# The turned x kept in memory by thirds, in place of turning it a second time

## The chip, the cores and the metric

The kernel runs on one core of one Trainium2 chip. The metric is the device time of one execution in microseconds. Engines are named as the profile names them: PE (TensorE), DVE (VectorE), ACT (ScalarE), POOL (GpSimd) and SP (SyncE, which only issues DMAs here).

## The reference, cut to what matters

```python
proj = x @ w_in                      # x: 1024 prompt + 128 sample tokens, 1024 wide
qa, ka, va, fa, qb, kb, vb, rb, a1, ga, gb = split(proj)
oa = fox_mixer(qa, ka, va, logsigmoid(fa + b_fgate), past)     # forgetting attention, 8 heads x 64
ya = oa @ w_a_out
ob = gla_mixer(qb, kb, vb, logsigmoid(a1 @ w_a2 + b_a2) / 16)  # gated linear attention, 4 heads
yb = (rms(ob) * g_gla * silu(rb)) @ w_b_out
x1 = LN(alpha * x + (sigmoid(ga) * ya + sigmoid(gb) * yb) @ w_o)
up = x1 @ w_up                        # then causal convolution, GEGLU, w_down, LN, per-layer embedding, LN
```

The prompt (1024 tokens) attends to itself; each of 8 sample streams (16 tokens each) attends to 256 cached keys and to its own. x is needed as the left side of every column of proj. The columns qa, ka, va, fa and a1 are computed ahead of the attention, all the others behind it.

## The kernel before, in words

Every float32 product is made of three matmuls: each operand is split into a part rounded to fp32r (`x_hi`) and the remainder (`x_lo`), and hi·hi, hi·lo and lo·hi are added in PSUM. ACT makes the rounded parts, DVE the remainders.

**x.** PE contracts over partitions, so x must lie with its 1024 features on partitions. For each of the 9 token tiles SP loads 128 rows (512 KB), PE turns them with 8 transposes of 128x128 (`turn_x`, L714 to L718), ACT copies the bank as `x_hi` (L1318, through L1300) and DVE subtracts for `x_lo` (L1901 to L1906). The two parts fill R1 and R2, each [128, 3 thirds, 8, 384 tokens]. A third is 3 tiles.

**Order of the work.** All is written out by hand, each engine its own program in order, and held together by semaphores. PE does: turn x, the columns of `w_in` that attention needs (loads 0 to 11, `load(n)`, L2905), then the prompt's attention head by head (`scores`, `probs_v`, L864), then the sample stage, then the gated linear attention (qb and kb first) and the rest. From the prompt's attention on, R1 and R2 hold that attention's operands, so x is gone when qb is wanted.

**The second turn.** SP therefore loads the 9 tiles of x again (`x_again`, L2996), the first four while the prompt's attention still runs, the others behind it, each as soon as its buffer is free. PE turns tile TURN_X2[0] behind the last `probs_v`, tiles 1 to 5 of that list inside the sample stage, and the last three (tiles 0, 1, 2: third 0) behind it. ACT and DVE split each again.

**The sample stage** (L946 to L960) is a loop over b = 0 to 10, software pipelined. In turn b PE does `past_keys(b+1)` (L886, 8 transposes), `sample_out(b-3)` (L934), a tile of x where 0 < b < 6, `sample_scores(b)` (L685, 20 matmuls with those of `sample_v`), `sample_turn(b-1)` (L920) and `sample_v(b-2)`. At b = 8, 9 and 10 a third of qb or kb is made (`QB_EARLY`), from thirds 2 and 1 of x. Then third 2 of kb, a wait for wa2 and for `s_a1`, and third 0 of qb and kb. `s_a1` comes from ACT, which copies the rank-16 input of the decay once POOL has stored the sample streams' output (L2761).

**PSUM.** It is four slots of two banks. `take` (L385 to L392) gives them out: with no slot named, use number i gets slot i modulo 4; before a use PE waits until every earlier use of that slot has been drained by its readers. `copied` waits for a use to have been drained, `past_pe` for PE to have filled it, `product` is the reader's side. The up projection is the first to name its slots: `first_half(0, 0)` asks for slot 0, `turn_x1(7)` for 3, `first_half(1, 0)` for 1. Just before it come, with no slot named, the alternating uses of the output projection and of the transposes of x1, in this order: wo(1, 6), x1T(4), wo(1, 7), x1T(5), wo(1, 8), x1T(6). The last two fall on slots 0 and 1: there are 514 uses before `first_half(0, 0)`, nine of which are the second turn's. DVE drains wo(1, 8) in L1882 (alpha·x added) and x1T(6) in L2345 (the remainder of x1's tile 6), which in its program comes behind the layer norm of tile 8.

Of the kernel before, what the change touches and what calls it, by code (L numbers as in the profile page):

```python
# [88 lines left out]
def build(nc, x_prompt, x_sample, cache_fox_k, cache_fox_v, cache_fox_logf, state_gla, cache_ffn_conv,  # L89
# [4 lines left out]
    with ctx:  # L94
# [149 lines left out]
        X_BUFS = 7  # L244
        xs = at(off["xs"], X_BUFS, 1024)

        TURN_X2 = [6, 7, 8, 3, 4, 5, 0, 1, 2]
        X2_HOME = {6: 0, 7: 1, 8: 2, 3: 3, 4: 4, 5: 0, 0: 1, 1: 2, 2: 3}
        x2_homes = [at(off["va"] + 1024 * i, 1024) for i in range(4)] + [at(off["qT"], 1024)]
        xs2 = [x2_homes[X2_HOME[n]] for n in range(NT)]  # L250
        qT, kT, va = at(off["qT"], 4, T), at(off["kT"], 4, T), at(off["va"], NT, 512)
        cwT = at(off["cw"], 4, 44)
        cacheT = at(off["cacheT"], 44, 16)
# [59 lines left out]
        x1h, x1l = rounded("x1_hi", off["x1h"], KT, T), rounded("x1_lo", off["x1l"], KT, T)  # L313
        g1, b1 = at(off["g1"], D), at(off["b1"], D)

        oa_out = nc.dram_tensor("branch_a", (P, 4, T), F32).ap()
        rs_out = nc.dram_tensor("row_sums", (H_A, SEQ), F32).ap()
        ri_out = nc.dram_tensor("row_scales", (H_A, SEQ), F32).ap()
# [217 lines left out]
        s_g1 = sem("ln_gains_in")  # L536

        s_xh1 = sem("x_hi_ready")
        s_sm = sem("small_hi_ready")
        s_sl = sem("small_lo_ready")  # L540
        s_obs = sem("branch_b_stored")
# [138 lines left out]
        def _(pe):  # L680
# [193 lines left out]
            turn_max(0)  # L874
            for u in range(3, 6):
                row_scores(1, u)
            def turn_again(n):
                pe.wait_ge(s_xt[n], 32)
                turn_x("xT2", n, xs2[n])

            def past_keys(b):
                pe.wait_ge(s_kp[b % 4], 16 * (b // 4 + 1))
# [52 lines left out]
                m.then_inc(filled(("soT", b)), 1)  # L935

            pe.wait_ge(s_ex, NT_S)
            turn_again(TURN_X2[0])
            pe.wait_ge(s_oe, 2 * H_A)
            pe.wait_ge(s_cols, 48)  # L940
            for b in range(DEC_B + 3):
                if 1 < b + 1 < DEC_B:
                    past_keys(b + 1)
                if b in QB_EARLY:
                    g = QB_EARLY[b]
                    copied(pe, *[("xT2", n) for n in range(3 * g, 3 * g + 3)])  # L946
                    thirds(("qb", 0), ("qb", 0), x_parts, only=(g,))
                if b == DEC_B + 2:
                    thirds(("kb", 0), ("kb", 0), x_parts, only=(1,))
                if b >= 3:  # L950
                    sample_out(b - 3)
                if 0 < b < 6:
                    turn_again(TURN_X2[b])
                if b < DEC_B:
                    sample_scores(b)
                if 1 <= b <= DEC_B:
                    sample_turn(b - 1)
                if 2 <= b <= DEC_B + 1:
                    sample_v(b - 2)
            for n in TURN_X2[6:]:  # L960
                turn_again(n)
            thirds(("kb", 0), ("kb", 0), x_parts, only=(2,))
            copied(pe, *[("xT2", n) for n in TURN_X2[6:]])

            pe.wait_ge(s_b, 16 * 2)
            pe.wait_ge(s_a1, 1)
# [323 lines left out]
        def _(act):  # L1290
# [106 lines left out]
            for q in range(2):  # L1397
                for n in range(NT):
                    o = product(act, ("va", q, n))
                    if q == 0:  # L1400
                        if n == 0:
                            act.wait_ge(s_nc0, 2)
                        copy(fat[:, n, 0:H_A], o[:, 256:256 + H_A])
                        copy(fat[:, n, 32:48], o[:, 256 + H_A:W_VF])
                    copy(va[:, n, q * 256:(q + 1) * 256], o[:, 0:256]).then_inc(drained(("va", q, n)), 1)
                    if (q, n) == (0, 2):
                        split_hi(11)
                    if (q, n) == (0, NT - 1):
                        forget_logs()
                    if (q, n) == (1, 1):  # L1410
                        decay_rank()
                    if (q, n) == (1, 2):
                        copied(act, *[("qa", 0, g) for g in range(3)])
                        qk_hi(0)

            def past_turned(b):
# [37 lines left out]
            for b in range(DEC_B + 1):  # L1454
                if 1 < b + 1 < DEC_B:
                    past_turned(b + 1)
                if b < 6:
                    x_hi("xT2", TURN_X2[b])
                if b in (DEC_B - 1, DEC_B):
                    split_hi(12 + b - DEC_B + 1)  # L1460
                if b >= 1:
                    o = product(act, ("spt", b - 1))
                    if b >= 3:
                        past_pe(act, ("spv", b - 3))
                    copy(sPT[:, (b - 1) % 2, :], o[:, 0:384]).then_inc(drained(("spt", b - 1)), 1)
                if b < DEC_B:
                    act.wait_ge(s_smx, b + 1)
                    if b >= 2:
                        past_pe(act, ("spt", b - 2))
                    o = product(act, ("ss", b))  # L1470
                    act.activation(sP[:, b % 2, 256:384], sN[b % 2], ACT.Exp, bias=nm[:, b % 2:b % 2 + 1],
                                   accum_out=rsb[:, b % 2:b % 2 + 1])
                    act.activation(sP[:, b % 2, 0:256], o[:, 0:256], ACT.Exp, bias=nm[:, b % 2:b % 2 + 1],
                                   accum_out=rs[:, b % 2:b % 2 + 1]).then_inc(s_exs, 1)
# [12 lines left out]
            split_hi(14)  # L1487
            qb_third(0, 1)
            copied(act, *[("spv", b) for b in range(DEC_B)])
            x_hi("xT2", *TURN_X2[6:])  # L1490
            copied(act, *[("soT", b) for b in range(DEC_B)])
            act.wait_ge(s_oao, 64)
            act.wait_ge(s_oas2, 32 * 2 * H_A + 16)
# [378 lines left out]
        def _(dve):  # L1872
# [162 lines left out]
            for b in range(DEC_B + 3):  # L2035
# [8 lines left out]
                if b >= 3:  # L2044
# [1 line left out]
                    t = 16 * (b - 3)  # L2046
                    dve.tensor_copy(oas[:, :, t:t + 16], o[:, 0:64].rearrange("p (j t) -> p j t", j=4))\
                        .then_inc(drained(("soT", b - 3)), 1)
                if b < 6:
                    x_lo("xT2", TURN_X2[b])  # L2050
                if b < DEC_B:
                    o = product(dve, ("ss", b))
                    q, qi = slice(b % 2, b % 2 + 1), slice(b % 4, b % 4 + 1)
# [20 lines left out]

            copied(dve, *[("soT", b) for b in range(DEC_B)])
            split_lo(14)
            x_lo("xT2", *TURN_X2[6:])
            kb_third(0, 2)

            dve.wait_ge(s_qbd, DEC_B)  # L2080
# [588 lines left out]
        def _(pool):  # L2669
# [5 lines left out]
            for i in range(2):  # L2675
                pool.memset(VH[i][:, :, DH:DH + 1].bitcast(F32), 1.0).then_inc(s_pz, 1)
                pool.memset(VL[i][:, :, DH:DH + 1].bitcast(F32), 0.0).then_inc(s_pz, 1)
            for i in range(3):
                pool.wait_ge(s_pz, 4 * i + 4)
                past_pe(pool, ("va", 1, 3 * i + 2))  # L2680
                pool.memset(sets[i][2][64:P, :].bitcast(F32), 0.0).then_inc(s_pz, 1)
                pool.memset(sets[i][3][64:P, :].bitcast(F32), 0.0).then_inc(s_pz, 1)
                pool.wait_ge(s_pz, 4 * i + 6)
                pool.memset(sets[i][2][64:66, :].bitcast(F32), 1.0).then_inc(s_pz, 1)
                pool.memset(sets[i][3][96:98, :].bitcast(F32), 1.0).then_inc(s_pz, 1)
# [77 lines left out]

            pool.wait_ge(s_oas2, 32 * 2 * H_A + 16)
            pool.wait_ge(s_oao, 64)
            past_pe(pool, *[("xT2", n) for n in range(NT)])
            pool.memset(qsm, 0.0).then_inc(s_pool, 1)
            for h in range(H_B):
                if h:
# [125 lines left out]
        def _(sp):  # L2895
# [33 lines left out]
            with nc.allow_non_contiguous_dma(reason="small columns"):  # L2929
# [3 lines left out]
                sp.dma_start(cwst[:, 0:3, :], conv_w[0].rearrange("j (c p) -> c j p", p=P)).then_inc(s_cv, 16)  # L2933
                sp.dma_start(cwst[:, 3, :], conv_b[0].rearrange("(c p) -> c p", p=P)).then_inc(s_cv, 16)
                sp.dma_start(lfp.rearrange("p (b n) h -> p b n h", n=2), cache_fox_logf[0].rearrange("b (n p) h -> p b n h", p=P)).then_inc(s_lf, 16)
            load(4)
            load(5)
            sp.dma_start(hc, consts[:, C_OMASK:C_SCAN]).then_inc(s_cols, 16)
            with nc.allow_non_contiguous_dma(reason="small columns"):
                sp.dma_start(ba2, b_a2[0].rearrange("(c p) -> p c", p=P)).then_inc(s_cols, 16)  # L2940
                sp.dma_start(ggla, g_gla[0].rearrange("(c p) -> p c", p=P)).then_inc(s_cols, 16)
                sp.dma_start(bfg, b_fgate[0].partition_broadcast(P)).then_inc(s_small, 16)
                past_pe(sp, "cacheT")
                for c, w, col in ((2 * P, H_A, O_F), (2 * P + H_A, RANK, O_A1)):
                    sp.dma_start(vfr[:, :, c:c + w], w_in[0].rearrange("(k p) n -> p k n", p=P)[:, :, col:col + w]).then_inc(s_small, 16)
            load(6)
            load(7)
            for n in range(8, 12):
                load(n)

            rows_p, rows_s = (lambda ap: ap[0, 0].rearrange("t h d -> t (h d)")), (lambda ap: ap[0].rearrange("b t h d -> (b t) (h d)"))
            def head_operands(h, parts="hl"):
# [15 lines left out]
                if "l" in parts:  # L2968
                    sp.wait_ge(s_lo, 2 * j + 2)
                    for dst, src in ((qq[DH:P], q_lo), (kc[0:DH], k_lo)):  # L2970
                        sp.dma_start(dst, src).then_inc(s_set[h % 3], 16)

            sp.wait_ge(s_ncl, 1)
            sp.wait_ge(s_hi, 3)
            head_operands(0, "h")
# [17 lines left out]
                    sp.dma_start(buf[b].rearrange("p (n c) -> p n c", n=2),  # L2993
                                 src[0, b].rearrange("(n p) h d -> p n (h d)", p=P)).then_inc(s[b % 4], 16)

            def x_again(*tiles):  # L2996
                for n in tiles:
                    sp.dma_start(xs2[n], tokens(x_prompt[0], x_sample, n)).then_inc(s_xt[n], 16)

            k_part, v_part = (kp, cache_fox_k, s_kp), (vp, cache_fox_v, s_vp)  # L3000
            for g in range(H_A):
# [15 lines left out]
            sp.wait_ge(s_s2, NS * (H_A - 1))  # L3017
            for b in range(4, 8):
                past(b, v_part)
            sp.wait_ge(s_vl, H_A)  # L3020
            sp.wait_ge(s_ov, 32)
            x_again(6, 7, 8, 3)
            sp.wait_ge(s_pv, NT_S)
            x_again(4)
            for n, after in ((5, 6), (0, 7), (1, 8), (2, 3)):
                past_pe(sp, ("xT2", after))
                x_again(n)
            past_pe(sp, ("spv", 3))
            load(14)
            load(15)  # L3030
            past_pe(sp, ("kpT", DEC_B - 1))
            load(12)
            load(13)
            copied(sp, *[("soT", b) for b in range(DEC_B)], ("spv", DEC_B - 1))
            sp.dma_start(wa2, w_a2[0]).then_inc(s_b, 16)
            sp.dma_start(scanm, consts[:, C_SCAN:C_ALL]).then_inc(s_b, 16)
# [168 lines left out]
```

## Time and profile before

| | |
|---|---|
| median of 3 runs | 2298.22 us (2296.01 to 2298.61) |
| the profiled execution | 2298.97 us |
| its span in the trace | 2297.2 us |
| mean granted clock | 0.991 |
| PE busy | 2236.4 us, 97% |
| DVE, ACT, POOL busy | 52%, 35%, 19% |
| DMA | 219.38 MB, 95 GB/s |

All stretches are us from the span's start. The prompt's attention lies at about 145 to 351, the sample stage at 351 to 446, the up projection begins at 1350.86. "Granted clock" is 1.00 where TensorE was given 2.4 GHz and 0.50 where it was given 1.2 GHz.

### The profile page before, as it was taken

How to read it: one execution, taken by the hardware profiler on the slowest of the kernel's cores; microseconds unless marked ns; L12 is line 12 of the kernel's file. 1: busy time of each engine (PE TensorE's matmuls, PEld its weight loads, DVE VectorE, ACT ScalarE, POOL GpSimd, SP SyncE). 2: the span in 40 equal slices, each digit the busy share in tenths (PEclk: the TensorE clock that was granted, in tenths of full speed). 3: DMA queues.
4: the chain of work that ended last, by engine and by line, in shares of the span. 5: the costliest groups of instructions: out<-in, count | busy, mean ns of one | idle time of the engine just before them, and what ended most of it. 6: DMA issues, size and time to landing. Idle time of an engine off the chain costs nothing.

```text
span 2297.2 us, 33210 instructions
## 1 busy us (share of the span) xinstructions
PE 2236.4 (97%) x13703; PEld 2065.8 (90%) x13703; DVE 1183.2 (52%) x1631; ACT 796.9 (35%) x1213; POOL 434.8 (19%) x537
## 2 busy tenths in 40 slices
PE   8999999999999999999999998999999999999997
PEld 8997777898999999999999888999999998888886
DVE  2226663263636363101533588666676766656446
ACT  3124664242425243112312024344444345333311
POOL 0001123001010101000032124354545420001011
PEclk9999999999999999999999999999999999999999
DMA  5109643301212121312323121222222249444420
GB/s 165 44 19 246 174 144 116 89 19 40 76 40 76 40 76 40 117 37 81 93 75 119 38 101 58 74 73 77 70 77 74 73 128 321 163 141 164 150 76 37
DMA packets 201004, 219.38 MB, mean 95 GB/s; under 512 B 40522, under 2 KB 161590, under 8 KB 200198
## 3 DMA queue, kind: packets, MB, share of 16 engines
q1 hardware_dynamic: 191846, 187.38, 26.9%
q0 software_dynamic: 9008, 29.87, 4.0%
q8 instruction: 109, 1.79, 0.3%
q14 instruction: 41, 0.34, 0.0%
HBM read 163.03 MB, written 41.53 MB: 89 GB/s over the span
## 4 chain that ended last, share of the span: by engine, by line
PE 87%; DVE 4%; SPq 2%; DMA 2%; issue 2%; ACT 1%; POOL 1%; DVEq 0%; POOLq 0%; ACTq 0%
PE ps L685 41%; PE ps L1166 19%; PE ps L1197 10%; PE ps L1245 4%; PE ps L1098 3%; PE ps L1009 2%; PE ps L864 1%; SPq L2967 1%; DVE sb L1882 1%; PE ps L824 1%; PE ps L717 1%; DVE sb L1986 1%; PE ps L1060 0%; PE ps L846 0%; PE ps L1039 0%
## 5 line engine op out<-in xcount | busy, mean ns | idle before, releaser
L685 PE MATMUL ps<-x_hi,ring_hi 128*128 128x384 f32 x960 | 326.9, 341 | 0.4 <-ACT sb L1300 0.4
L685 PE MATMUL ps<-x_hi,ring_lo 128*128 128x384 f32 x960 | 321.5, 335 | 0.0
L685 PE MATMUL ps<-x_lo,ring_hi 128*128 128x384 f32 x960 | 321.5, 335 | 0.0
L1300 ACT ACTIVATE sb<-ps 128x64 f32<-128x64 f32 (+8 forms) x235 | 106.1, 473 | 351.9 <-PE ps L685 218.2
L1896 DVE TENSOR_TENSOR ring_lo<-ring_raw,ring_hi 128x1024 fp32r<-128x1024 f32 (+1 forms) x66 | 76.0, 1158 | 210.1 <-ACT ring_hi L1300 209.2
L685 PEld LDWEIGHTS ps<-x_hi,ring_hi 128*128 128x128 f32 x960 | 180.7, 188 | 3.8 <-issue 3.5
L685 PEld LDWEIGHTS ps<-x_lo,ring_hi 128*128 128x128 f32 x960 | 180.9, 188 | 1.0 <-issue 0.7
L685 PEld LDWEIGHTS ps<-x_hi,ring_lo 128*128 128x128 f32 x960 | 180.7, 188 | 0.0
L1197 PE MATMUL ps<-down_hi,h_hi 128*128 128x512 f32 x396 | 155.6, 393 | 0.5 <-DVE h_lo L2475 0.4
L1197 PE MATMUL ps<-down_hi,h_lo 128*128 128x512 f32 x396 | 154.3, 390 | 0.0
L1197 PE MATMUL ps<-down_lo,h_hi 128*128 128x512 f32 x396 | 154.2, 389 | 0.0
L1882 DVE SCALAR_TENSOR_TENSOR convolved_halves<-sb,convolved_halves 128x1168 f32<-128x1168 f32 x88 | 127.0, 1444 | 35.5 <-ACT convolved_halves L1713 32.8
L2813 POOL TENSOR_SCALAR sb<-sb 128x1 f32<-128x1 f32 x27 | 35.4, 1312 | 443.9 <-DVE sb L2323 435.0
L2473 DVE TENSOR_TENSOR down_lo<-down_raw,down_hi 128x1024 fp32r<-128x1024 f32 x66 | 80.6, 1221 | 59.8 <-ACT down_hi L1300 59.6
L1713 ACT ACTIVATE convolved_halves<-sb 128x1168 f32<-128x1168 f32 x44 | 60.0, 1367 | 144.2 <-issue 92.0
L1882 DVE SCALAR_TENSOR_TENSOR sb<-sb 128x1024 f32<-128x1024 f32 (+5 forms) x79 | 87.5, 1118 | 38.1 <-ACT sb L1516 24.4
L685 PE MATMUL ps<-ring_hi,x_hi 128*128 128x256 f32 x360 | 104.9, 291 | 0.0
L685 PE MATMUL ps<-sb 128*128 128x256 f32 (+4 forms) x400 | 101.8, 391 | 0.1
L685 PE MATMUL ps<-ring_hi,x_lo 128*128 128x256 f32 x360 | 101.8, 283 | 0.0
L685 PE MATMUL ps<-ring_lo,x_hi 128*128 128x256 f32 x360 | 101.7, 283 | 0.0
L1300 ACT ACTIVATE down_hi<-down_raw 128x1024 fp32r<-128x1024 f32 x66 | 69.7, 1056 | 71.9 <-DMA down_raw<-in_w_down 71.8
L1882 DVE SCALAR_TENSOR_TENSOR sb<-sb,ps 128x256 f32<-128x256 f32 (+2 forms) x87 | 49.8, 595 | 79.5 <-PE ps L1098 43.8
(353 smaller groups left out, 5722.3 us busy)
## 6 DMA issues: line engine op xcount, KB each, us to landing
down_raw<-in_w_down SPq DMA_DIRECT2D x66, 512.0 KB, 3.7
ring_raw<-in_w_in SPq DMA_DIRECT2D x50, 512.0 KB, 3.9
h_raw<-h_chunks SPq DMA_DIRECT2D x66, 192.0 KB, 3.8
sb<-in_x_prompt SPq DMA_DIRECT2D x24, 512.0 KB, 7.9
h_chunks<-convolved_halves SPq DMA_DIRECT2D x22, 512.0 KB, 2.8
up_raw_b<-in_w_up SPq DMA_DIRECT2D x38, 256.0 KB, 3.8
up_raw<-in_w_up SPq DMA_DIRECT2D x34, 256.0 KB, 3.0
branch_b<-sb POOLq DMA_DIRECT2D x4, 1152.0 KB, 7.2
```

What stands on the lines that cost most here:

```text
L685: m = mm(out, l, r, start=(n == 0), stop=(n == len(pairs) - 1))
L1009: m = mm(o[:, n * w:(n + 1) * w], a[:, t], later(c, t, l), start=True, stop=True)
L1098: m = mm(o[:, 0:512], a, b, start=(k == i == 0), stop=(k == KT - 1 and i == 2))
L1166: m = mm(o[:, 512 * j:512 * j + BW], a, b[:, BW * j:BW * (j + 1)], start=(not more and k == n == 0), stop=(k == 3 and n == 2), skip_group_ ...
L1197: m = mm(o[:, cc], a, b, start=(k == e == 0), stop=(k == LAST and e == 2), skip_group_check=True)
L1245: m = mm(o, l, r, start=(k == e == 0), stop=(k == KT - 1 and e == 2))
L1300: return act.activation(out, in_, ACT.Copy, scale=scale)
L1713: act.activation(y[:, v, 0:1168], U[:, v, 0:1168], ACT.Identity, bias=cwT[:, 3, n:n + 1], scale=cwT[:, 0, n:n + 1])\
L1882: return dve.scalar_tensor_tensor(out=out, in0=in0, scalar=scalar, in1=in1, op0=op0, op1=op1)
L1896: dve.tensor_tensor(ringl[:, i, 0:kt], ring[:, i, 0:kt], ringh[:, i, 0:kt].bitcast(F32), ALU.subtract)\
L2473: dve.tensor_tensor(wdl[s % WD_SLOTS], rawd[s % WD_SLOTS], wdh[s % WD_SLOTS].bitcast(F32), ALU.subtract).then_inc(s_dl, 1)
L2813: pool.tensor_scalar(lve[:, q:q + 1], mv[:, q, 1:2], LN_EPS, None, ALU.add).then_inc(s_msq, 1)
```

## The change: what it does

After x has been turned the first time, SP stores both parts to a scratch tensor in device memory, six stores of 1536 KB (12,288 contiguous bytes in each of 128 partitions). Those who write over R1 and R2 later (ACT before `qk_hi(0)`, POOL before the memsets of the sets, SP before `head_operands`) first wait for all six. The second loads, transposes and splits go. SP loads the parts back instead: thirds 2 and 1 behind the last probabilities of the prompt's attention (each: hi whole, lo in two halves), third 0 in three pieces behind `spv` 5, 6 and 7. PE waits for the landings (`x_back`) where it waited for the splits.

```diff
+        x_out = nc.dram_tensor("x_parts", (2, 3, P, KT, THIRD), F32).ap()
...
-            def turn_again(n):
-                pe.wait_ge(s_xt[n], 32)
-                turn_x("xT2", n, xs2[n])
+            def x_back(g):
+                for n in range(3 * g, 3 * g + 3):
+                    pe.wait_ge(s_xt[n], 32)
...
             pe.wait_ge(s_ex, NT_S)
-            turn_again(TURN_X2[0])
             pe.wait_ge(s_oe, 2 * H_A)
...
                 if b in QB_EARLY:
                     g = QB_EARLY[b]
-                    copied(pe, *[("xT2", n) for n in range(3 * g, 3 * g + 3)])
+                    x_back(g)
                     thirds(("qb", 0), ("qb", 0), x_parts, only=(g,))
...
-                if 0 < b < 6:
-                    turn_again(TURN_X2[b])
...
-            for n in TURN_X2[6:]:
-                turn_again(n)
             thirds(("kb", 0), ("kb", 0), x_parts, only=(2,))
-            copied(pe, *[("xT2", n) for n in TURN_X2[6:]])
+            x_back(0)
...
# ACT
+                        act.wait_ge(s_xst, 96)
                         qk_hi(0)
...
-                if b < 6:
-                    x_hi("xT2", TURN_X2[b])
...
-            x_hi("xT2", *TURN_X2[6:])
...
# DVE
-                if b < 6:
-                    x_lo("xT2", TURN_X2[b])
...
-            x_lo("xT2", *TURN_X2[6:])
...
# POOL
+            pool.wait_ge(s_xst, 96)
...
-            past_pe(pool, *[("xT2", n) for n in range(NT)])
...
# SP
+            def x_away(g):
+                copied(sp, *[("xT", n) for n in range(3 * g, 3 * g + 3)])
+                for i, a in enumerate((xh, xl)):
+                    sp.dma_start(x_out[i, g], a[:, g].bitcast(F32)).then_inc(s_xst, 16)
...
+            x_away(0)
             load(6)
             load(7)
+            x_away(1)
+            x_away(2)
...
+            sp.wait_ge(s_xst, 96)
             sp.wait_ge(s_ncl, 1)
             sp.wait_ge(s_hi, 3)
             head_operands(0, "h")
...
-            def x_again(*tiles):
-                for n in tiles:
-                    sp.dma_start(xs2[n], tokens(x_prompt[0], x_sample, n)).then_inc(s_xt[n], 16)
+            def x_in_again(i, g, k0, k1, n):
+                sp.dma_start((xh, xl)[i][:, g, k0:k1].bitcast(F32), x_out[i, g, :, k0:k1]).then_inc(s_xt[n], 16)
...
-            sp.wait_ge(s_vl, H_A)
-            sp.wait_ge(s_ov, 32)
-            x_again(6, 7, 8, 3)
             sp.wait_ge(s_pv, NT_S)
-            x_again(4)
-            for n, after in ((5, 6), (0, 7), (1, 8), (2, 3)):
-                past_pe(sp, ("xT2", after))
-                x_again(n)
+            for g in (2, 1):
+                x_in_again(0, g, 0, KT, 3 * g)
+                x_in_again(1, g, 0, KT // 2, 3 * g + 1)
+                x_in_again(1, g, KT // 2, KT, 3 * g + 2)
...
+            past_pe(sp, ("spv", 5))
+            x_in_again(0, 0, 0, KT // 2, 0)
+            past_pe(sp, ("spv", 6))
+            x_in_again(0, 0, KT // 2, KT, 1)
+            past_pe(sp, ("spv", 7))
+            x_in_again(1, 0, 0, KT, 2)
             copied(sp, *[("soT", b) for b in range(DEC_B)], ("spv", DEC_B - 1))
             sp.dma_start(wa2, w_a2[0]).then_inc(s_b, 16)
             sp.dma_start(scanm, consts[:, C_SCAN:C_ALL]).then_inc(s_b, 16)
```

## Rows read from the trace of the kernel before

**Rows 1.** The page, part 4: the chain that ended last, shares by engine.

```profile
PE 87%; DVE 4%; SPq 2%; DMA 2%; issue 2%; ACT 1%; POOL 1%; DVEq 0%; POOLq 0%; ACTq 0%
```

**Rows 2.** Chain of waits, end of the prompt's attention: start us, us, what.

```profile
339.99 5.40 DMA row_sums<-sb
...
351.00 0.90 PE ps L717 x8
351.89 3.91 PE ps L685 x20
```

**Rows 3.** Timeline of ACT there: start, us, operation [idle before <-releaser].

```profile
345.48 0.60 ACT L1300 ACTIVATE sb<-ps 65x512 f32<-65x512 f32 x1 [2.02 <-DMA row_sums<-sb]
...
351.03 0.59 ACT L1300 ACTIVATE sb<-ps 65x512 f32<-65x512 f32 x1 [0.42 <-PE ps L864]
```

**Rows 4.** DMA view, whole span: issues, KB each, median us to landing.

```profile
row_sums<-sb POOLq DMA_DIRECT2D x16, 2.0 KB, 2.6
...
ob_raw<-branch_b POOLq DMA_DIRECT2D x3, 1536.0 KB, 7.3
```

**Rows 5.** Chain of waits, sample stage.

```profile
356.82 0.87 PE ps L717 x8
...
390.81 0.87 PE ps L886 x8
...
400.69 0.87 PE ps L886 x8
...
407.15 2.59 PE ps L685 x6
...
439.15 2.66 PE ps L717 x24
```

**Rows 6.** Timeline of PE, from the attention's end to the sample stage's.

```profile
349.04 0.45 PE L864 MATMUL ps<-p_hi,v_hi 128*65 128x512 f32 x1 [0.92 <-DVE p_lo L1999]
...
362.74 1.04 PE L717 MATMUL ps<-sb 128*128 128x128 f32 x8
...
446.34 0.41 PE L685 MATMUL ps<-x_hi,ring_hi 128*128 128x384 f32 x1 [0.36 <-ACT sb L1300]
```

**Rows 7.** Timeline of POOL, the same.

```profile
358.26 0.52 POOL L2724 COPY sb<-sb 64x64 f32<-64x64 f32 x2
...
439.95 0.75 POOL L2761 DMA_DIRECT2D branch_a<-sb  x1 [41.74 <-DVE sb L2047]
```

**Rows 8.** Timeline of ACT at the stage's end.

```profile
444.79 1.16 ACT L1300 ACTIVATE sb<-sb 16x1152 f32<-16x1152 f32 x1 [1.75 <-DMA branch_a<-sb]
```

**Rows 9.** Chain of waits, from 74.85.

```profile
74.85 35.19 PE ps L685 x203
```

**Rows 10.** Timeline of SP's queue there.

```profile
87.53 12.85 SPq L2905 DMA_DIRECT2D vf_raw<-in_w_in  x2
```

**Rows 11.** Timeline of DVE at the start of the up projection.

```profile
1356.45 1.22 DVE L2345 TENSOR_TENSOR x_lo<-ps,x_hi 128x1024 fp32r<-128x1024 f32 x1
```

**Rows 12.** Chain of waits there.

```profile
1350.86 5.96 PE ps L685 x48
...
1361.73 19.62 PE ps L685 x168
```

**Rows 13.** Timeline of PE: first matmuls behind two gaps.

```profile
191.29 0.33 PE L824 MATMUL ps<-kk,qq 128*128 128x128 f32 x1 [1.78 <-DMA kc<-k_lo]
...
1414.85 0.82 PE L1166 MATMUL ps<-x_hi,up_hi 128*128 128x288 f32 x2 [8.02 <-ACT sb L1300]
```

**Rows 14.** Windows: stretch, length, busy us of PE, PEld, DVE, ACT, POOL, granted clock, DMA share, GB/s.

```profile
192.00:194.00 2.00, 2.00 (x10) 1.57 (x9) 1.22 (x3) 1.27 (x2) 0.00 (x0) 0.50 1.05 392
194.00:196.00 2.00, 2.00 (x11) 1.43 (x8) 0.18 (x2) 0.85 (x1) 0.00 (x0) 0.68 1.02 371
...
1414.00:1420.00 6.00, 5.15 (x21) 5.18 (x22) 5.96 (x5) 4.11 (x9) 0.00 (x0) 0.50 0.13 40
1420.00:1422.00 2.00, 2.00 (x14) 2.00 (x14) 2.00 (x5) 1.08 (x2) 1.72 (x3) 0.83 0.03 8
```

More of the change, by code:

```diff
@@ L245, in build @@
         xs = at(off["xs"], X_BUFS, 1024)
[L247 to L250, printed above, removed]
         qT, kT, va = at(off["qT"], 4, T), at(off["kT"], 4, T), at(off["va"], NT, 512)
@@ L538, in build @@
         s_xh1 = sem("x_hi_ready")
+        s_xst = sem("x_parts_stored")
         s_sm = sem("small_hi_ready")
```

## The prediction, made before the changed kernel ran

> **What bounds the kernel now.** I read the page first. The chain that ended last is 87% PE, so a microsecond counts where it lengthens or shortens what PE does or waits for [rows 1]. Next came the chain of waits over the two stretches that the diff touches, the end of the prompt's attention with the sample stage, and the start of the up projection. The reader is to see that all transposes of the second turn (L717) but one tile's lie on that chain, in one piece with PE's other work [rows 2, 5], and that two waits stand beside them: PE's 0.92 us for the last probabilities [rows 6] and the 0.36 us ahead of third 0 of qb [rows 6]. Then the timelines of ACT, POOL and DVE, for what each of these waits is behind. Last, the granted clock behind PE's gaps [rows 14], since the change makes new gaps. A change under 0.2% (4.6 us) can't be told from none in this kernel.
>
> **The early stores.** Six stores of 1536 KB go out from SP at about 60 to 80 us. The nearest row is the read back of 1536 KB, 7.3 us [rows 4]; six at that rate one behind the other are 44 us, the upper end. load(6) and load(7) share the engines with them, and 8 to 11 stand behind them in SP's program, but loads 8 and 9 wait for PE anyway, at 87.53 and 12.85 us later [rows 10], while PE works unbroken for 35.19 us from 74.85 [rows 9]. x_away(0), 15 us by that row, ends near 75, and the other four, 29 us, near 104 at the slowest. Nothing of R1 and R2 is overwritten before the attention begins at 145. The waits for s_xst on ACT, POOL and SP hold up nothing then. Cost 0; ends 0 and, if load(9) came behind the last stores, about 3 us. I take 0, since row after row of this stretch shows PE ahead of nothing but its own work.
>
> **The end of the attention.** SP no longer reads four tiles of x beside the last stores of the attention's output. Before, row_sums landed after 5.40 us [rows 2], against a median of 2.6 [rows 4]; ACT waited 2.02 us for it [rows 3], and behind ACT and DVE PE waited 0.92 us [rows 6]. 5.40 less 2.6 is 2.8, more than the 2.02, so ACT's wait goes and PE's with it: **-0.92**, ends -0.92 and 0. What is late next is PE itself.
>
> The first tile of the second turn (0.90 us [rows 2]) goes, but PE then waits for ACT's copy of the last output chunk, which ends at 351.03 + 0.59 = 351.62, against 351.89 when the next matmuls began [rows 2, 3]. With some 0.07 us for the release **-0.2** remains.
>
> **The sample stage, tiles 1 to 5 of the list.** Tile 1 is 0.87 us of chain [rows 5]. Tile 2 is 1.04 us of PE [rows 6], ahead of matmuls that the chain shows waiting for DVE: ss(2) has by rotation the slot of ss(1), four uses earlier. With the turn gone it has another slot and waits only for POOL's sample_queries(2). Together **-1.91**, ends 0 and -2.1. Tiles 3, 4 and 5: the turn with a tile lasts 400.69 - 390.81 = 9.88 us, the turn without one, b = 6, 407.15 + 2.59 - 400.69 = 9.05 [rows 5], so 0.83 each and **-2.49**. The splits that go from ACT and DVE were beside PE. Sum up to here: -0.92 - 0.2 - 1.91 - 2.49 = **-5.52**.
>
> **The reloads.** Thirds 2 and 1 are 6.3 MB behind the last probabilities, at about 350. By the row, 4 times 7.3 = 29 us one behind the other at the most [rows 4], so landed by 380; they are wanted at b = 8, past 409 [rows 5]. Hidden. The remainder of third 0 is issued behind spv(7), which ends one kb third (4.17 us, below) and under 1 us of L934 before 439.15 [rows 5], so about 434.1, or 428.6 with the 5.5 us saved; 7.3 us later it is 435.9. PE wants it at 437.8. Hidden, with 2 us over. What the reloads cost is contention: POOL's small stores and loads of the attention's last chunk now run beside 6.3 MB. sample_queries(2) ran from 358.26 to 358.78 [rows 7]; ss(2) would begin in place of the transposes at 362.74 [rows 6], less the 2.0 us saved before it, 360.7: 1.9 us of slack. I take **+0.3**, between 0 and +3.8 (rival D). Here the trace says that small transfers beside large ones took 5.40 us where 2.6 is usual [rows 2, 4]. The Trainium skill, "DMA: Bandwidth & Descriptors", section "Issuing engines are not separate DMA queues", has it that DMAs started by different engines run on the same 16 DMA engines and interleave: the change moves this collision from 340 to 350, it doesn't end it. By that rule alone the sum would lean to D.
>
> **The last three tiles.** Their 2.66 us [rows 5] go, and PE gains nothing. Behind soT(7), which ended at 439.15, there is a second path: DVE copies, POOL stores branch_a at 439.95 [rows 7], it lands, ACT makes its copy, 444.79 + 1.16 = 445.95 [rows 8], and third 0 of qb begins at 446.34 [rows 6]. PE's own path was 2.66 and kb's third 2, 446.34 - 0.36 - 439.15 - 2.66 = 4.17 us. Without the transposes PE is ready at 439.15 + 4.17 = 443.32 and waits 3.02 us. Gain **0**; ends 0 and -1, if the store lands sooner without its neighbours.
>
> **The clock behind that wait.** After a gap of 1.78 us [rows 13] the granted clock was 0.50 and 0.68 in the next two stretches of 2 us [rows 14]: 2 x 0.50 + 2 x 0.32 = 1.6 us lost. After one of 8.02 us [rows 13] it was 0.50 to 1420 and 0.83 to 1422: 5.15 x 0.50 + 2 x 0.17 = 2.9 us lost. For 3.0 us I take **+1.7**, near the shorter gap; ends 0 and +2.9. This is a new cost.
>
> **What the diff moves without naming it: the slots.** Nine uses of PSUM with no slot named go. Uses with no slot named wait for the one four before them, whatever the start, but the up projection names its slots. Before it there were 514 uses: wo(1, 8) had slot 0 and x1T(6) slot 1. With 505 all shift by one (nine less is one less modulo 4): x1T(6) gets slot 0 and wo(1, 8) slot 3. first_half(0, 0) asks for slot 0. Before, it waited for DVE to drain wo(1, 8) and began at 1350.86 [rows 12]. Now it waits for the remainder of x1's tile 6, which DVE makes at 1356.45 for 1.22 us [rows 11], behind tile 8's layer norm, which does not depend on first_half. 1357.67 + 0.04 - 1350.86 = **+6.85**; ends 0 (if I have miscounted the slots) and +6.85. Queued behind the waiting PE instruction is the whole first column, 5.96 us and later 19.62 us of matmuls [rows 12], on whose end SP's next load of w_up waits, and through that the sums that PE waited 8.02 us for at 1414.85 [rows 13]. That wait starts from PE too, so it absorbs nothing. The clock behind a gap of 7.0 us, by the row of 8.02: **+2.9**; ends +1.6 and +2.9.
>
> **Sum.** -5.52 + 0.3 + 0 + 1.7 + 6.85 + 2.9 = +6.2 us. The profiled execution took 2298.97, its span 2297.2: 2305.2. The median of the three runs lies 0.75 us below the profiled one, so the forecast is **2304.4 us**, slower by 0.27%.
>
> **Rivals.** (A) The forecast. Its own range is 2302 to 2307: the clock terms 1.7 and 2.9 each within some 1.3 us, the saving of tile 2 within 1.
>
> (B) The slots cost nothing, since DVE has x1's tile 6 ready or another use holds slot 0. Then 2298.22 - 5.52 + 0.3 + 1.7 = 2294.7, faster by 0.15%, or 2293.0 and faster by 0.23% if the 3.0 us wait leaves the clock alone. For it: only that all the changed lines lie a millisecond ahead. Against: DVE's program puts the tile behind tile 8's norm, and the timeline shows that order [rows 11].
>
> (C) The slot wait comes but the rest is kinder: the clock is not lowered behind the wait at 440 and only 1.6 us are lost behind the one at 1351, or the branch_a chain shortens by 1. Then 2298.22 - 5.52 + 0.3 + 6.85 + 1.6 = 2301.5, less up to 1: 2300.5 to 2302.5, no change that can be told. For it: the two falls that the rows show differ, 1.6 and 2.9 us, so the size behind a given gap is not certain [rows 14]. Against: both gaps were followed by one.
>
> (D) The bulk reload takes the place of the x loads as the thing that POOL's transfers collide with. POOL waits for two of them in a row before sample_queries(2); each 2.8 us longer (5.40 less 2.6 [rows 2, 4]) is 5.6, less 2 us of slack: ss(2) is 3.6 to 3.8 us late, in place of the 0.3. 2304.4 + 3.5 = 2307.9. It decides from the point at which POOL's delay exceeds 2 us. For it: 6.3 MB go in one piece where four tiles (2 MB) did the damage. Against: of those transfers one at most lay on the path before.
>
> **How the numbers follow.** A 0.50, C 0.28, D 0.15, B 0.07. Slower by over 0.2% (above 2302.8): D and nearly all of A, 0.63. Within 0.2%: C, the rest of A, and a part of B, since 2294.7 is less than 4.6 us below before: 0.32. Faster (below 2293.6): 0.05. The range of 8 in 10 takes A, C and most of D: 2298.5 to 2308.5; B and D's tail lie outside.
>
> **What would show it.** Right: at about 1345 (1350.86 less 5.5 and plus the clock) PE idle for 7 us before the first `x_hi,up_hi` matmul, released by DVE's L2345 of before, and a granted clock of 0.50 after it; PE idle for about 3 us ahead of third 0 of qb, released by ACT's 16x1152 copy; row_sums landing in under 3.6 us at the attention's end; and turns of 9.05 us in the sample stage throughout. Wrong: an unchanged start of the up projection relative to what precedes it (B); a PE gap between 352 and 365 released by POOL or a DMA (D); a granted clock of 1.00 behind both gaps (C).

## The result and the profile after

The changed kernel took 2301.26 us (median of 17 runs, 2299.28 to 2307.03) against 2298.18 us for the kernel before (17 runs, 2296.01 to 2299.63): a ratio of 1.0014, 95% interval 1.0008 to 1.0021. It is slower by 3.1 us, clear of zero but inside the 0.2% that the prediction calls no change: a case to which it gave 0.32, against 0.63 for slower by more. Forecast were 2304.4 us, +6.2; the measured time lies in the range of 8 in 10 (2298.5 to 2308.5), and just below the 2302 to 2307 that the forecast gave as its own. The profiled execution took 2300.44 us, its span 2298.7: 1.5 us more than the profile of before.

First the chain of waits of the changed kernel over the attention's end and the sample stage (start us, us, what). `L862`, `L683`, `L884` and `L932` are the old `L864`, `L685`, `L886` and `L934`.

```profile
348.42 1.74 PE ps L862 x12
350.16 0.73 issue
350.89 4.09 PE ps L683 x20
...
386.20 0.87 PE ps L884 x8
...
395.25 0.88 PE ps L884 x8
...
432.93 0.81 PE ps L932 x8
433.74 0.02 issue
433.77 0.24 DVE sb L2038
...
434.57 4.70 DMA branch_a<-sb
```

PE ends the attention at 350.16, where it was 351.00 [rows 2]; the sample stage's first matmuls start 1.00 us sooner; a turn of the loop now takes 395.25 - 386.20 = 9.05 us; and the last `sample_out` ends at 433.74 in place of 439.15 [rows 5], 5.41 us sooner. (The two executions were already 0.31 us apart before these stretches, by an ACT copy at 338.57 before and 338.88 after; counted from there the attention's end gains 1.15 us and the whole 5.72.) Behind it the chain no longer runs through PE but through the store of `branch_a`. The timelines of ACT and of PE show the two waits concerned:

```profile
343.67 0.58 ACT L1293 ACTIVATE sb<-ps 65x512 f32<-65x512 f32 x1
```

```profile
440.90 0.41 PE L683 MATMUL ps<-x_hi,ring_hi 128*128 128x384 f32 x1 [2.91 <-ACT sb L1293]
```

ACT's copy of the output chunk has no idle time before it any more (2.02 us in [rows 3]; row_sums landed in 2.6 us, where it had taken 5.40), and third 0 of qb starts 5.44 us sooner than in [rows 6], but behind a wait of 2.91 us for ACT's 16x1152 copy.

Then the start of the up projection, by the timelines of DVE and PE:

```profile
1349.81 1.28 DVE L1873 SCALAR_TENSOR_TENSOR sb<-sb 128x1024 f32<-128x1024 f32 x1 [0.46 <-POOL sb L2803]
1351.01 1.22 DVE L2333 TENSOR_TENSOR x_lo<-ps,x_hi 128x1024 fp32r<-128x1024 f32 x1
```

```profile
1352.38 0.55 PE L683 MATMUL ps<-x_hi,up_hi 128*128 128x256 f32 x1 [7.14 <-DVE x_lo L2333]
```

Tile 6's remainder (answering [rows 11]) ends 5.44 us sooner than before, like all that precedes it. PE is idle for 7.14 us until then, and starts 1.52 us later than in [rows 12]. Relative to the 5.44 us saved, the slot costs 6.96 us.

Last the granted clock, by windows (stretch, length, busy us of PE, PEld, DVE, ACT, POOL, granted clock, DMA share, GB/s): of the changed kernel behind both gaps and behind a later gap of 8.02 us, which [rows 13] has in the kernel before; and of the kernel before in one stretch that the prediction did not look at.

```profile
440.00:442.00 2.00, 1.10 (x4) 1.13 (x5) 0.00 (x0) 0.54 (x1) 2.00 (x3) 0.81 0.06 8
442.00:444.00 2.00, 2.00 (x8) 2.00 (x8) 0.00 (x0) 0.00 (x0) 0.30 (x1) 0.50 0.92 293
444.00:446.00 2.00, 2.00 (x11) 2.00 (x10) 0.00 (x0) 0.00 (x0) 0.00 (x0) 0.83 0.66 223
...
1350.00:1352.00 2.00, 0.00 (x0) 0.00 (x0) 2.00 (x2) 0.00 (x0) 1.15 (x1) 0.50 0.69 279
1352.00:1354.00 2.00, 1.62 (x7) 1.65 (x8) 0.23 (x1) 0.00 (x0) 0.00 (x0) 0.50 0.60 246
1354.00:1356.00 2.00, 2.00 (x11) 2.00 (x11) 0.00 (x0) 0.00 (x0) 0.00 (x0) 0.50 0.00 0
1356.00:1358.00 2.00, 2.00 (x18) 2.00 (x18) 0.00 (x0) 0.00 (x0) 0.00 (x0) 0.99 0.00 0
...
1416.00:1418.00 2.00, 0.33 (x1) 0.36 (x2) 2.00 (x2) 2.00 (x5) 0.00 (x0) 0.50 0.82 246
1418.00:1420.00 2.00, 2.00 (x10) 2.00 (x10) 2.00 (x2) 2.00 (x6) 0.00 (x0) 0.50 0.00 0
1420.00:1422.00 2.00, 2.00 (x14) 2.00 (x14) 1.97 (x3) 0.94 (x1) 0.00 (x0) 0.78 0.00 0
```

```profile
458.00:460.00 2.00, 2.00 (x8) 2.00 (x7) 0.00 (x0) 1.97 (x2) 0.00 (x0) 0.53 0.03 8
460.00:462.00 2.00, 2.00 (x9) 2.00 (x9) 0.00 (x0) 1.97 (x3) 0.00 (x0) 0.62 0.00 0
```

PE went on at 1.2 GHz behind both new gaps, as forecast. But behind the 7.14 us gap the clock, low already while PE still waited, stayed low for only some 3.6 us of work. Behind the gap of 8.02 us, which both kernels have, 1.6 us were lost in the changed kernel (0.33 x 0.50 + 2 x 0.50 + 2 x 0.22) and 2.9 in the kernel before, by the prediction's own sum: the loss behind one and the same gap is not fixed. And the execution profiled of the kernel before had a fall of its own, at 458 to 462, which the changed kernel's has not. It cost about what the changed kernel's fall at 440 cost, and so the two profiles are as far apart ahead of the up projection as at 440 (5.44 us).

### The profile page after: what moved, and what is told of

Same layout as the page of the kernel before. It is cut to its first block, busy times and chain, and to the rows that moved or that the text cites. A ratio compares the mean times of both kernels' runs of the same rounds, so it can differ in the third digit from the quotient of the medians.

```text
span 2298.7 us, 33044 instructions
## 1 busy us (share of the span) xinstructions
PE 2227.6 (97%) x13631; PEld 2057.7 (90%) x13631; DVE 1172.9 (51%) x1622; ACT 787.6 (34%) x1204; POOL 434.7 (19%) x537
## 4 chain that ended last, share of the span: by engine, by line
PE 87%; DVE 4%; SPq 2%; DMA 2%; issue 2%; POOL 1%; ACT 1%; DVEq 0%; POOLq 0%; ACTq 0%
PE ps L683 40%; PE ps L1159 19%; PE ps L1190 10%; PE ps L1238 4%; PE ps L1091 3%; PE ps L1002 2%; PE ps L862 2%; PE ps L844 1%; SPq L2963 1%; PE ps L822 1%; DVE sb L1873 1%; PE ps L845 1%; PE ps L1053 0%; DVE sb L1977 0%; DMA kc<-k_lo 0%
## 5 line engine op out<-in xcount | busy, mean ns | idle before, releaser
L683 PE MATMUL ps<-x_hi,ring_hi 128*128 128x384 f32 x960 | 326.8, 340 | 2.9 <-ACT sb L1293 2.9
L683 PE MATMUL ps<-x_hi,ring_lo 128*128 128x384 f32 x960 | 321.7, 335 | 0.0
L683 PE MATMUL ps<-x_lo,ring_hi 128*128 128x384 f32 x960 | 321.4, 335 | 0.0
L683 PEld LDWEIGHTS ps<-x_hi,ring_hi 128*128 128x128 f32 x960 | 181.0, 189 | 6.4 <-issue 6.1
L683 PEld LDWEIGHTS ps<-x_lo,ring_hi 128*128 128x128 f32 x960 | 180.8, 188 | 0.9 <-issue 0.7
L683 PEld LDWEIGHTS ps<-x_hi,ring_lo 128*128 128x128 f32 x960 | 180.7, 188 | 0.0
L683 PE MATMUL ps<-ring_hi,x_hi 128*128 128x256 f32 x360 | 104.9, 291 | 0.0
L683 PE MATMUL ps<-sb 128*128 128x256 f32 (+4 forms) x400 | 102.0, 391 | 0.7 <-issue 0.7
L683 PE MATMUL ps<-ring_hi,x_lo 128*128 128x256 f32 x360 | 101.8, 283 | 0.0
L683 PE MATMUL ps<-ring_lo,x_hi 128*128 128x256 f32 x360 | 101.7, 283 | 0.0
```

The source lines that it names most:

```text
L683: m = mm(out, l, r, start=(n == 0), stop=(n == len(pairs) - 1))
```

## The experiments

All are timed against the kernel before on the same chip. Of "after" and "before", each is the starting point named.

**e1: the slots put back.** Edit on the changed kernel:

```diff
             x_back(0)
+            turn["slot left out"] = None
```

> The changed kernel with one number left out of the slot count behind the sample stage, so that every later PSUM use has the slot that it had in the kernel before. Theory (slots): first_half(0, 0) waits again for DVE's L1873 and not for x1's tile 6; the 7 us gap ahead of the up projection and the slower clock behind it go, and the time is that of the kernel before less the 5.4 us saved by the sample stage: 2293 us, about 8 us under the changed kernel, ratio to before 0.9977. Rival (traffic or something else late in the kernel holds x1's tile 6): the gap stays, 2301.

Measured: 2294.31 us (11 runs), ratio 0.9982 (0.9973 to 0.9991). The start of the up projection in its timeline of PE:

```profile
1351.70 0.36 PE L683 MATMUL ps<-x_hi,up_hi 128*128 128x256 f32 x1 [0.17 <-DVE sb L1874]
```

One dictionary entry that stands for no work takes 7.0 us off the median and turns the change from slightly slower to slightly faster than the kernel before. The gap goes to 0.17 us. The rival is out. The gain over the kernel before is 4.0 us, not 5.4; this profile fell on the slowest of the eleven executions, which e5 comes back to.

**e2: the slots alone.** Edit on the kernel before, which keeps its second turn:

```diff
             copied(pe, *[("xT2", n) for n in TURN_X2[6:]])
+            for i in range(3):
+                turn["slot left out", i] = None
```

> The kernel before with three numbers left out of the slot count behind the sample stage (three more is one less modulo four): nothing else is changed. Theory (slots): first_half(0, 0) starts 7.0 us later than in the kernel before, released by DVE L2345, and the whole takes 7 to 8.3 us more: 2305 to 2306.5 us. Rival (the gap comes from the reloads or stores): no gap, 2298.

Measured: 2305.93 us (5 runs), ratio 1.0032 (1.0019 to 1.0045), 7.65 us slower. Its timeline of PE:

```profile
1357.41 0.55 PE L685 MATMUL ps<-x_hi,up_hi 128*128 128x256 f32 x1 [7.15 <-DVE x_lo L2347]
```

The gap is there with none of the change's transfers. With e1 this shows that the change's whole loss is the slots' shift. It costs the gap of 7 us; the median leaves about 0.7 us for the clock behind it, where 2.9 had been set, though five runs with this interval (4.4 to 10.3 us) don't fix so small a term.

**e3: the wait behind third 0.** Edit on e1:

```diff
-            pe.wait_ge(s_b, 16 * 2)
-            pe.wait_ge(s_a1, 1)
             for h in range(H_B):
                 if h == 0:
                     thirds(("qb", h), ("qb", h), x_parts, only=(0,))
                     thirds(("kb", h), ("kb", h), x_parts, only=(0,))
+                    pe.wait_ge(s_b, 16 * 2)
+                    pe.wait_ge(s_a1, 1)
```

> e1 with PE's wait for wa2 and for the rank-16 input (s_b, s_a1) moved behind third 0 of qb and kb, which need neither. Theory (the 3 us wait is that of the stored branch_a, and the clock fell because of it): PE runs on at about 437.7, 3.0 us come off and with them the fall of the clock at 440, 1.7 us: 2288.5 us. Rival (the fall is due anyway and only changes its place, as it did from 458 to 440 between the two kernels): 3.0 us come off and a fall of about 1.7 us stands somewhere before 465: 2290. Rival 2 (third 0 lands too late): a wait on the DMA x_lo<-x_parts takes its place, 2292.

Measured: 2292.07 us (5 runs, 2285.29 to 2292.36), ratio 0.9961 (0.9949 to 0.9974). The chain runs through PE alone from the last `sample_out` to the decay's matmuls (L967), with no fall of the clock:

```profile
430.23 0.80 PE ps L932 x8
431.03 12.58 PE ps L683 x72
443.61 2.13 PE ps L967 x6
```

That is 12.58 us, where the changed kernel took from 433.74 to 451.03, 17.29: 4.7 us less, the wait and the clock. Third 0 was there in time. But the median is only 2.2 us under e1's, while the profiled execution, the fastest of the five, is 9 us under it. Five executions that spread over 7 us don't size this; e6 repeats it.

**e4: loads for nobody.** Edit on the changed kernel:

```diff
             for b in range(4, 8):
                 past(b, v_part)
+            sp.wait_ge(s_vl, H_A)
+            sp.wait_ge(s_ov, 32)
+            for i, n in enumerate((6, 7, 8, 3)):
+                sp.dma_start(at(off["va"] + 1024 * i, 1024), tokens(x_prompt[0], x_sample, n)).then_inc(s_dup, 16)
             sp.wait_ge(s_pv, NT_S)
...
+            sp.wait_ge(s_dup, 64)
             sp.dma_start(wa2, w_a2[0]).then_inc(s_b, 16)
```

> The changed kernel, which also loads four tiles of x at the place of the old second load, into the same places, and nobody reads them. Theory (those loads delayed row_sums and through ACT the end of the attention): row_sums lands after about 5.4 us again, ACT waits for it some 2 us, and PE's last probs_v ends about 0.8 us later than in the changed kernel, at 351.0. Rival (PE's earlier end has another cause): it ends at 350.2 as in the changed kernel, with row_sums landing in under 3 us.

One execution: 2301.59 us, which tells nothing by itself. Its chain and its timeline of ACT:

```profile
340.04 5.60 DMA row_sums<-sb
```

```profile
345.72 0.59 ACT L1294 ACTIVATE sb<-ps 65x512 f32<-65x512 f32 x1 [2.21 <-DMA row_sums<-sb]
```

ACT's wait is back, and PE's for the last probabilities too: 1.02 us, which neither the changed kernel nor e1 has at that place. The last `probs_v` ends at 351.26, 1.1 us later than in the changed kernel. The loads did delay the attention's end, and what it gained (0.84 us by the two profiles, 1.15 counted from ACT's copy before it) is theirs.

**e5: a later reload.** Edit on e3:

```diff
-            sp.wait_ge(s_pv, NT_S)
+            past_pe(sp, ("spv", 1))
             for g in (2, 1):
                 x_in_again(0, g, 0, KT, 3 * g)
```

> e3 with the reload of thirds 2 and 1 issued behind spv(1) in place of right behind the attention's last probabilities (some 25 us later; they are wanted 30 us after that). Theory (the reload's traffic slows POOL's transfers, and only their slack hides it; where it is used up, DVE's wait for row_sums holds ss(2) and PE): the load of row_sums lands in 2 to 3 us in place of 8 to 9, DVE's wait for it in the sample stage goes, the slow single runs of this family (2298 and 2307 where 2294 and 2301 are usual) go, and the median stays within 1 us of e3's. Rival (the traffic costs nothing, its neighbours neither): the landings stay long, no difference to e3 in median or in spread. Rival 2 (too late): PE waits for x_lo<-x_parts at b = 8, +1 to 3 us.

Measured: 2288.25 us (5 runs, 2286.51 to 2291.39), ratio 0.996 (0.9948 to 0.9973). What it was about shows in the DMA view of the stretch behind the attention, for the changed kernel and then for e5 (issues, KB each, us to landing):

```profile
x_hi<-x_parts SPq DMA_DIRECT2D x2, 1536.0 KB, 10.8
x_lo<-x_parts SPq DMA_DIRECT2D x4, 768.0 KB, 13.6
...
row_sums<-sb POOLq DMA_DIRECT2D x1, 2.0 KB, 6.1
sb<-row_sums POOLq DMA_DIRECT2D x1, 8.0 KB, 8.2
```

```profile
row_sums<-sb POOLq DMA_DIRECT2D x1, 2.0 KB, 1.9
sb<-row_sums POOLq DMA_DIRECT2D x1, 8.0 KB, 3.7
```

8 KB took 8.2 us beside the bulk reload and 3.7 without it (4.6 in the kernel before). In the changed kernel DVE waited for it, ahead of the work on ss(2):

```profile
366.28 0.25 DVE L1995 RECIPROCAL sb<-sb 128x16 f32<-128x16 f32 x1 [3.89 <-DMA sb<-row_sums]
```

That wait is gone in e5. In time there is no difference to e3 that these runs can show: 2288.25 against e6's 2288.42. The delay lay in slack. It did not always: the profiled execution of e1, the slowest of its eleven at 2298.76 us, shows this chain:

```profile
358.52 9.33 DMA sb<-row_sums
...
367.94 0.06 DVE sb L1996
...
370.42 1.03 PE ps L932 x8
...
379.24 1.87 DVE sb L2060
...
382.29 6.81 PE ps L683 x20
```

The landing took 9.33 us, 1.1 us more than in the changed kernel; DVE, which takes its program in order, came late to ss(2), and PE waited 1.07 us ahead of L932. The second wait, of 1.92 us, has another last link. DVE, by now late, met POOL's multiplication:

```profile
378.75 2.34 POOL L2699 TENSOR_TENSOR sb<-sb 128x1024 f32<-128x1024 f32 x1 [4.55 <-DMA sb<-row_scales]
379.16 1.94 DVE L2060 TENSOR_TENSOR sb<-sb 128x1 f32<-128x1 f32 x1
```

The DVE instruction on 128x1 elements takes 0.15 us in the same turn of the changed kernel, where it starts at 377.87 and POOL's multiplication at 377.90. Here it started 0.41 us behind POOL's and ended with it, which reads as DVE being held up until POOL was done; no run isolates that. After that PE worked at the lower clock from 382 on (6.81 us for 20 matmuls that take 3.95). From the attention's end to the last `sample_out` this execution took 91.1 us, the changed kernel's 83.6: 7.5 us more. This is rival D, in one execution, and at twice its price. e4 stands at its edge: there the landing took 8.64 us and PE waited 0.29 us ahead of its L933, where 0.13 is usual. Whether e5 is free of it, five runs don't tell.

**e6 and e7: e3 and e1 once more, beside e5.**

> e3 once more, beside e5 and e1 on the same chip. The profile of e3 had the 3.0 us and no slower clock at 440, 4.7 us less than the changed kernel there, and yet its median stood 2.2 us under e1's. Theory (the slower clock behind the 3 us wait comes in some executions only, and others come by chance elsewhere): 3 to 4.7 us under e1, some 2290 us. Rival (the slower clock comes later in its place): about 2 to 3 us under e1, with a fall between 440 and 465 in the profile.

> e1 once more, on the same chip as e5 and e6; its profile fell on a run of 2298.76 us where the other ten had 2293.0 to 2295.4. Theory: 2294 us; a profile without PE's waits of 1 and 2 us ahead of L932 at 370 and 381, and with the 2.9 us wait for ACT's 16x1152 copy, released at about 440.6. Rival (those waits belong to every run of the changed sample stage): they stand again.

Measured: e6 2288.42 us (5 runs, 2286.32 to 2289.38), ratio 0.9956 (0.9943 to 0.9968); e7 2294.08 us (11 runs, 2291.24 to 2298.90), ratio 0.9985 (0.9976 to 0.9994). The chains at the sample stage's end, e7 and then e6:

```profile
432.32 0.81 PE ps L932 x8
...
440.22 8.59 PE ps L683 x48
```

```profile
432.58 0.80 PE ps L932 x8
433.38 12.58 PE ps L683 x72
```

In e7 third 0 of qb starts behind a wait of 2.84 us, and its 48 matmuls take 8.59 us, full speed: no fall of the clock. Of the four profiles with this wait, two had the fall (the changed kernel and e4, 1.6 us) and two had not (e1, e7). The profiled executions of e6 and e7 differ by 2.9 us in span (2286.6 and 2289.5), about the wait alone. By medians e3 stands 2.2 us under e1 and e6 5.7 us under e7; taken together, the ten executions with the wait moved have a median of 2288.9 us and the 22 without it 2294.2, 5.3 us apart. So moving the wait gains the 3 us of the wait itself, and perhaps 2 more. How much of the rest is clock stays open, since falls elsewhere differ between executions: at the start of the attention, between 190 and 208, the clock was at 0.50 for about 3.4 us in e3's profile and for about 13.6 us in e6's and e7's, by the granted clock of the 2 us windows. The rival, a fall that comes later in its place, is not seen before 465 in e3, e5 or e6. The waits ahead of L932 at 370 and 381 are not in e7's profile, so they don't belong to every execution; two of e7's eleven took 2298.6 and 2298.9, as e1's slow one did, and have no profile.

## Why the prediction was right and where its sizes were wrong

Mechanism and sign were right; the forecast was twice the measured +3.1 us, and what doubled it are the two clock terms. By its steps:

- **Early stores: 0.** Right. They took 6.1 to 17.6 us to land, the last at about 95.4, and PE's unbroken stretch of L685, of which [rows 9] shows a piece, runs from 62.56 for 93.06 us (before from 62.54 for 93.06).
- **Attention's end: -0.92 and -0.2.** It gave 0.84 and, with the first transposes, 1.00 in all (1.31 counted from ACT's copy at 338), against 1.12. e4 shows the cause.
- **Tiles 1 to 5: -1.91 and -2.49.** With the two terms above this gave 5.41 (5.72 counted from ACT's copy), against 5.52 in all. A turn of the loop took the 9.05 us that I expected.
- **Contention: +0.3.** Not on PE's path in the usual execution, though the landings were longer than I had set: 10.8 us for 1536 KB (median), and 8.2 for POOL's 8 KB. In e1's slow execution it cost 7.5 us, twice what D charged, because a collision of DVE with POOL and a fall of the clock came on top, which D did not have. How often that happens, the runs leave open.
- **The last three tiles: 0.** Right: a wait of 2.91 us in place of 3.02, on the chain that was named. e3 and e6 took it away.
- **The slots: +6.85.** 6.96 in the profile; e2 has it alone. The part of the prediction that no line of the diff names was the largest, and among the most exact.
- **The clock: +1.7 and +2.9.** These two terms failed. For the first, the fall of 1.6 us did come in the profile of the changed kernel, but it comes in some executions only, and the profile of before, from which the sum starts, had one of the same size at 458 which I left out of the balance. For the second, I took the loss behind the 8.02 us gap as a fixed price. Behind the 7.14 us gap the work up to 1364.56 took 1.31 us more than before, not 2.9. That the clock was low during part of the gap does not explain the difference: in the row that I used it was, too (0.61 at 1410 to 1412, with PE idle). The low stretch was simply shorter, as it was in the changed kernel behind the very gap of 8.02 us (1.6 us lost in place of 2.9); why, no run shows. Further on 1.4 us came back, 0.98 of them in the 144 matmuls behind the gap at 1441 (21.01 us against 21.99). By e2's median the slots with all their clock cost 7.65, and by e1's 7.0.

Put together for the profiled pair: -5.44 + 6.96 + 1.31 = +2.83 at 1364.56, less 1.4 later, +1.5 in span. With medians: -4.0 (e1) + 7.0, about +3.1. The clock was charged 4.6 us in the forecast. Between the two profiles none of it is left: -5.44 + 6.96 is the whole +1.5. Summed over each span in windows of 2 us (PE's busy time times one less the granted clock), it took an estimated 12.5 us before and 11.8 in the changed kernel. The medians leave 3.1 - 1.5 = 1.6 us, which no profile assigns. Measured at 2301.26, the time fell among C's numbers (2300.5 to 2302.5). C's condition held in part only: less was lost behind the later gap, but the clock did fall at 440 in the profile, and what cancelled it was the fall of the kernel before, which no rival named. That it came out inside C is partly luck.

e3, e5 and e6 beat the kernel before by about 0.4% and the changed one by about 0.5%; the version to keep is the change with its slot count restored and the wait moved (e3, e6), with or without the later reload.

## What to carry to other kernels

Where buffers are handed out by counting, removing uses moves every later use; look for the first place that names its buffer, and check who drains what is there. A step taken off the engine that bounds the kernel gives nothing where a second chain starts at the same point: ask what else must arrive, and move the wait behind work that doesn't need it. Falls of the clock behind one and the same gap differ from execution to execution; charge for one a range and not a price, count only the work that PE does in it, and set it against those that the profile of before has by chance.

## What the runs showed of the hardware

A gap of PE of 2.8 to 3.1 us was followed by a granted clock of 0.50 in two profiles (the changed kernel, e4) and by 1.00 throughout in two others (e1, e7). Behind the 7.14 us gap it was 0.50 before PE resumed. Behind a gap of 8.02 us at the same place of the program 2.9 us were lost in the kernel before and 1.6 in the changed one. An 8 KB load took 8.2 us beside a reload of 6.3 MB (the changed kernel), and 3.7 us without it (e5). A DVE instruction on 128x1 elements with both inputs in SBUF took 1.94 us while POOL multiplied 128x1024 elements in SBUF, and 0.15 us in the changed kernel, where it started just ahead of POOL's. A reciprocal of the same size, with one input, took 0.16 us while POOL's multiplication ran (the changed kernel, at 378.05). That POOL held the first up is read from one execution (e1).
